# Two places where TensorE waits for a split: the head of the down projections, and the attended parts of the cross attention, taken in another order

## The chip, the cores and the metric

The kernel runs on one core of one Trainium2 chip. The time is device microseconds (us) of one execution on that core, as the median of three runs.

## The reference

512 tokens of width 1024 go through two blocks of two layers each; all data are float32. What matters here is the feed-forward part of each of the four layers and the cross attention of the last two:

```
# first block, for l in range(2)
up = h2 @ w_up[l]; a, v = up[..., :2816], up[..., 2816:]
x = x + (gelu(causal_depthwise_conv(a, conv_w[l], conv_b[l])) * v) @ w_down[l]

# second block, for layer in range(2)
q = h @ wq;  k, v = split(mem_n @ wkv)              # 4 heads of 128; 256 memory rows
p = softmax(einsum('bshd,bmhd->bhsm', q, k) * 128 ** -0.5)
x = x + einsum('bhsm,bmhd->bshd', p, v).reshape(B, S, 512) @ wo
g, u = split(h @ w_gate_up);  x = x + (silu(g) * u) @ w_down
```

## The kernel before

**Products.** Activations lie feature-major: a tile is 128 features x 512 tokens. To keep float32 accuracy at the speed of the shorter format, every operand is split in two: hi, a rounded copy, and lo, the rest. `product` (L706) makes three matmuls for each tile of the contraction, hi x hi, lo x hi and hi x lo (L711 to L713), all into one PSUM bank. M is a set of four such banks, M0 to M3, and A another.

**Weights** come in chunks. SyncE loads a chunk into `stage` (two parts); ScalarE makes w_hi (`split_hi`, L1500, the activation at L1507) when the chunk two before has been used (`w_used`), and VectorE makes w_lo (`split_lo`, L2118, at L2122). w_lo's end (`w_lo_done`) lets TensorE start (`chunk_in`, L732) and lets SyncE load the next chunk into the freed part of `stage`. Chunks alternate between two slots for their halves w_hi and w_lo, and between the banks M0, M1 and M2, M3. `m_free` tells that a bank pair was read out. The order of work on each engine is the order of the code; nothing else sets it.

**Feed-forward** (L828 on TensorE, L1630 on ScalarE, L2233 on VectorE). The 22 hidden tiles are done in two halves, of 12 and of 10. In a half, each up chunk gives one tile of each branch in two banks. VectorE scales both (L2242, L2244), the convolution runs on ScalarE and VectorE (L1640, L2252; not in layers 2 and 3), VectorE makes the w_lo of a later chunk, ScalarE the activation, VectorE the product `hid` (L2260), ScalarE `hid_hi` (L1651), and VectorE `hid_lo` (L2262), which counts up `hid_lo_done`. Then eight down chunks follow, one for each of the 8 output tiles, over the half's 12 or 10 hidden tiles: even ones into M0, odd ones into M2. In the first of them `hidden_as_split` waits for each hidden tile's hid_lo; the last hidden tile is the last of its contraction. When a down chunk is used, VectorE adds its bank to x (L2269, or L2206 in second halves, where squares for the next norm and the split of x follow), and the weights two chunks on are split.

**Cross attention** (L1138, L1833, L2609; layers 0 and 1 of the second block, whose feed-forward parts are the kernel's layers 2 and 3). Four heads. For each: scores (`score`), the row maxima and `normalise` on VectorE, the exponentials `exps` on ScalarE (L1850), the transposes `turn` (L1165) of the probabilities on TensorE, their copy `back` (L1858), and `value` (L1173), whose result is split by ScalarE (`attended_hi`, L1864) and VectorE (`attended_lo`, L2650, counting up `at_out`) into xo_hi and xo_lo. The output projection is made of parts: `part(n, k)` is head k's share of output pair n, six matmuls. Heads 0 and 1 are in the banks A while heads 2 and 3 use the banks M. TensorE's order around the change is value(0), value(1), turn(2), part(0, 0), part(0, 1), turn(3), part(1, 0), part(1, 1), value(2), value(3), and the rest of the parts. The parts with n = 2 and 3 use the second output chunk, whose w_lo VectorE makes in this stretch (`split_after(c0 + 1, 1)`).

Of the kernel before, what the change touches and what calls it, by code (L numbers as in the profile page):

```python
# [33 lines left out]
KT = D // P  # L34
# [132 lines left out]
def block_program(nc, dram, out):  # L167
# [7 lines left out]
    for l in range(2 * DEPTH):  # L175
        for half, (_, n) in enumerate(HALVES):
            c0, count = start[f"down{l}{half}"]
            size[c0:c0 + count] = [n // 2 * P] * count

    with ExitStack() as ctx:  # L180
# [524 lines left out]
        def _(pe):  # L705
            def product(bank, lhs, rhs, k, k0=0, k1=None):  # L706

                last = None
                for n in range(k0, k if k1 is None else k1):
                    (a_hi, a_lo), (b_hi, b_lo) = lhs(n), rhs(n)  # L710
                    pe.matmul(bank, a_hi, b_hi, start=(n == 0), stop=False)  # L711
                    pe.matmul(bank, a_hi, b_lo, start=False, stop=False)  # L712
                    last = pe.matmul(bank, a_lo, b_hi, start=False, stop=(n == k - 1))  # L713
                return last
# [17 lines left out]
            def chunk_in(c):  # L732

                pe.wait_ge(w_lo_done, c * 2 + 2)
                pe.wait_ge(m_free, c + 1)
# [83 lines left out]
            def turn_result(k):  # L819

                pe.wait_ge(normed_done, normed_tiles_before(LAST_NORM) + k + 1)
                if k >= 2:
                    pe.wait_ge(out_ready, k - 1)
                for t in range(TT):
                    last = pe.transpose(A[k % 2][:, t * P:(t + 1) * P], gained[:, k % 2, t * P:(t + 1) * P], ident)
                last.then_inc(out_turned, 1)

            def feed_forward(l, n_norm):  # L828
                for half, (f0, n) in enumerate(HALVES):
                    c0 = start[f"up{l}{half}"][0]  # L830
                    if half == 0:
                        normed_tiles(f"up{l}0", n_norm)
                    else:
                        with pe.Fori(0, n // 2) as i:
                            for s in range(2):
                                two_tiles(i * 2 + (c0 + s), s, normal, KT)
                    c0 = start[f"down{l}{half}"][0]

                    def down_weight(s):
                        def at(k):  # L840
                            o = (k // (n // 2)) * HALF + (k % (n // 2)) * P
                            return w_hi[:, s, o:o + P], w_lo[:, s, o:o + P]
                        return at

                    def hidden_as_split(k):

                        pe.wait_ge(hid_lo_done, up_counts(l, half) + k + 1)
                        return hidden(k)
                    if half == 1 and l == 2 * DEPTH - 1:
                        for j in range(KT):  # L850
                            chunk_in(c0 + j)
                            product(M[2 * (j % 2)][:, :], down_weight(j % 2), hidden if j else hidden_as_split, n).then_inc(w_used, 1)
                            if j:
                                turn_result(j - 1)
                        break
                    chunk_in(c0)
                    product(M[0][:, :], down_weight(0), hidden_as_split, n).then_inc(w_used, 1)
                    chunk_in(c0 + 1)
                    product(M[2][:, :], down_weight(1), hidden, n).then_inc(w_used, 1)
                    with pe.Fori(1, KT // 2) as i:  # L860
                        for s in range(2):
                            chunk_in(i * 2 + (c0 + s))
                            product(M[2 * s][:, :], down_weight(s), hidden, n).then_inc(w_used, 1)
# [635 lines left out]
        def _(act):  # L1499
# [333 lines left out]
            def cross_attention(l):  # L1833

                n0 = AT0[f"x{l}"]
                c0 = start[f"xkv{l}"][0]
                split_after(c0, 0)
                split_after(c0 + 1, 1)
                norm_rows(XATTN[l])
                split_after(c0 + 2, 0)  # L1840
                split_after(c0 + 3, 1)
                c0 = start[f"xq{l}"][0]
                split_after(c0, 0)

                def exps(h):

                    act.wait_ge(at_max, n0 + h + 1)
                    for i in range(TT):
                        j = 4 * (h % 2) + i
                        last = act.activation(x_prob[:, h % 2, i * N_MEM:(i + 1) * N_MEM], cross_scores(h, i), ACT.Exp,  # L1850
                                              bias=neg_max[:, j:j + 1], scale=P ** -0.5, accum_out=soft_den[:, j:j + 1])
                    last.then_inc(at_exp, 1)

                def back(h):

                    act.wait_ge(at_turned, n0 + h + 1)
                    for kt in range(N_MEM // P):
                        last = act.activation(x_turned[:, h % 2, kt * S:(kt + 1) * S], cross_banks[h][kt][:, :], ACT.Copy)  # L1858
                    last.then_inc(at_back, 1)

                def attended_hi(h):

                    act.wait_ge(at_pv, n0 + h + 1)
                    act.activation(xo_hi[:, h, :], cross_banks[h][0][:, :], ACT.Copy).then_inc(at_hi, 1)  # L1864

                exps(0)
                exps(1)
                back(0)
                back(1)
                split_after(c0 + 1, 1)  # L1870
                exps(2)
                exps(3)
                attended_hi(0)
                attended_hi(1)
                back(2)
                back(3)
                attended_hi(2)
                attended_hi(3)
                o0 = start[f"xo{l}"][0]
                for n in range(4):  # L1880
                    if n % 2:
                        split_hi(o0 + n // 2 + 2, n // 2)
                    if n < 2:
                        act.wait_ge(xo_added, 2 * l + n + 1)
                    else:
                        act.wait_ge(m_free, o0 + n + 1)
                    for m in range(2):
                        squared(FFN[l], 2 * n + m, m)
                        gained_hi(FFN[l], 2 * n + m)
                norm_rows(FFN[l])  # L1890
                feed_forward(2 + l, "silu", MIX[1] if l == 0 else LAST_NORM)
# [225 lines left out]
        def _(dve):  # L2117
# [8 lines left out]
            def split_after(c, s):  # L2126
                if c + 2 < chunks:
                    split_lo(c + 2, s, size[c + 2])
# [480 lines left out]
            def cross_attention(l):  # L2609
# [51 lines left out]
                maxima(2)  # L2661
                maxima(3)
                normalise(2)
                split_after(c0 + 1, 1)
                attended_lo(0)
                attended_lo(1)
                normalise(3)
                attended_lo(2)
                attended_lo(3)
                o0 = start[f"xo{l}"][0]  # L2670
# [349 lines left out]
```

## Time and profile before

| | |
|---|---|
| median of three runs | 2816.53 us |
| lowest and highest run | 2813.05 and 2818.16 us |
| span of the profiled execution, first to last instruction | 2808.1 us |
| around that span, if the profiled execution took the median | 8.4 us |
| TensorE matmuls, busy | 2745.4 us (98%) |
| VectorE, busy | 1535.5 us (55%) |
| ScalarE, busy | 1110.5 us (40%) |
| mean granted clock of TensorE | 0.994 |

The profile is of one execution, and its own whole time isn't listed beside its span; so sums are made against the span, and what lies around it is taken as the difference to the median.
### The profile page before, as it was taken

To read this page: it belongs to the slowest core of one execution; us is meant where nothing else is said; L and a number is where in the kernel's file an instruction comes from. 1 tells how busy PE (TensorE), PEld (TensorE's weight loads), DVE (VectorE), ACT (ScalarE), POOL (GpSimd) and SP (SyncE) were. 2 spreads that over 40 slices of the span, in tenths; PEclk is the share of its full clock that TensorE was granted. 3 is DMA by queue.
4 is the path that set the end of the run, shared out by engine and by line. 5 is a ranking of instruction groups with operands and counts; after the bars stand their busy time and mean duration, and the time that the engine had idled before them with its cause. 6 is when DMAs were issued, how large, how long until landed. Compare 5 with 4: busy or idle time off the path is not lost.

```text
span 2808.1 us, 33678 instructions
## 1 busy us (share of the span) xinstructions
PE 2745.4 (98%) x12745; PEld 2242.2 (80%) x12745; DVE 1535.5 (55%) x2107; ACT 1110.5 (40%) x1521; POOL 42.7 (2%) x36
## 2 busy tenths in 40 slices
PE   8999999999999999999999999999999889999998
PEld 7887788887888778888788878888878568788886
DVE  5376855456536685544667654434663545644444
ACT  3246544334313644433442443322443644533223
POOL 3000000000200000000000000000000000000000
PEclk9999999999999999999999999999999999999999
DMA  5321233332332123333243423333332114232332
GB/s 160 90 64 57 85 96 86 101 97 85 102 97 76 45 72 94 105 90 105 79 120 90 128 68 91 93 101 99 95 90 62 31 57 124 60 101 86 105 86 86
DMA packets 463902, 249.89 MB, mean 89 GB/s; under 512 B 21094, under 2 KB 459327, under 8 KB 463679
## 3 DMA queue, kind: packets, MB, share of 16 engines
q1 hardware_dynamic: 463807, 248.57, 30.9%
q8 instruction: 66, 1.08, 0.2%
q14 instruction: 29, 0.24, 0.0%
HBM read 246.44 MB, written 2.10 MB: 89 GB/s over the span
## 4 chain that ended last, share of the span: by engine, by line
PE 88%; DVE 6%; ACT 3%; issue 1%; DMA 1%; DVEq 0%; ACTq 0%; SPq 0%
PE M L711 26%; PE M L713 25%; PE M L712 25%; DVE w_lo L2122 1%; PE M L806 1%; PE M L804 1%; PE M L805 1%; PE A L901 1%; PE A L711 1%; PE A L876 1%; PE A L712 1%; PE A L713 1%; PE A L945 1%; PE A L890 0%; DVE prob L2565 0%
## 5 line engine op out<-in xcount | busy, mean ns | idle before, releaser
L711 PE MATMUL M<-h_hi,w_hi 128*128 128x512 f32 x2184 | 861.2, 394 | 3.6 <-DVE w_lo L2122 2.3
L713 PE MATMUL M<-h_hi,w_lo 128*128 128x512 f32 x2184 | 851.8, 390 | 0.0
L712 PE MATMUL M<-h_lo,w_hi 128*128 128x512 f32 x2184 | 851.7, 390 | 0.0
L1507 ACT ACTIVATE w_hi<-stage 128x1024 fp32r<-128x1024 f32 (+3 forms) x504 | 495.7, 1026 | 732.6 <-PE M L713 665.6
L2122 DVE TENSOR_TENSOR w_lo<-stage,w_hi 128x1024 fp32r<-128x1024 f32 (+3 forms) x504 | 586.8, 1202 | 149.9 <-ACT w_hi L1507 148.9
L711 PEld LDWEIGHTS M<-h_hi,w_hi 128*128 128x128 f32 x2184 | 410.8, 188 | 95.3 <-issue 5.9
L713 PEld LDWEIGHTS M<-h_hi,w_lo 128*128 128x128 f32 x2184 | 410.6, 188 | 86.7
L712 PEld LDWEIGHTS M<-h_lo,w_hi 128*128 128x128 f32 x2184 | 410.7, 188 | 86.4 <-issue 2.6
L711 PE MATMUL M<-hid_hi,w_hi 128*128 128x512 f32 x704 | 275.2, 391 | 7.0 <-DVE hid_lo L2262 7.0
L712 PE MATMUL M<-hid_lo,w_hi 128*128 128x512 f32 x704 | 274.0, 389 | 0.0
L713 PE MATMUL M<-hid_hi,w_lo 128*128 128x512 f32 x704 | 274.0, 389 | 0.0
L2242 DVE TENSOR_TENSOR normed<-M,rstd 128x512 f32<-128x512 f32 x88 | 60.9, 692 | 306.0 <-PE M L713 280.1
L711 PEld LDWEIGHTS M<-hid_hi,w_hi 128*128 128x128 f32 x704 | 132.1, 188 | 36.6 <-DVE hid_lo L2262 9.6
L713 PEld LDWEIGHTS M<-hid_hi,w_lo 128*128 128x128 f32 x704 | 132.2, 188 | 27.7
L712 PEld LDWEIGHTS M<-hid_lo,w_hi 128*128 128x128 f32 x704 | 132.1, 188 | 27.1
L1651 ACT ACTIVATE hid_hi<-hid 128x512 f32 x88 | 55.6, 632 | 180.8 <-DVE hid L2260 180.8
L2269 DVE TENSOR_TENSOR x<-x,M 128x512 f32 (+1 forms) x40 | 27.5, 688 | 165.0 <-PE M L713 165.0
L1648 ACT ACTIVATE acted<-normed 128x512 f32<-128x512 f32 x44 | 27.8, 632 | 223.8 <-DVE normed L2242 223.8
L2262 DVE TENSOR_TENSOR hid_lo<-hid,hid_hi 128x512 f32 x88 | 61.0, 693 | 82.6 <-ACT hid_hi L1651 82.6
L1640 ACT ACTIVATE conv<-normed,vec 128x512 f32<-128x512 f32 x44 | 35.9, 817 | 140.4 <-DVE normed L2242 140.2
L2252 DVE SCALAR_TENSOR_TENSOR conv<-normed,vec,conv 128x511 f32<-128x511 f32 x88 | 66.1, 751 | 46.2 <-ACT conv L1640 39.9
L2206 DVE TENSOR_TENSOR x<-x,M 128x512 f32 (+1 forms) x53 | 35.1, 683 | 85.0 <-PE M L713 83.5
(491 smaller groups left out, 3235.4 us busy)
## 6 DMA issues: line engine op xcount, KB each, us to landing
stage<-in_w_up SPq DMA_DIRECT2D x88, 512.0 KB, 4.5
stage<-in_ffn_w_gate_up SPq DMA_DIRECT2D x88, 512.0 KB, 4.8
stage<-in_w_in SPq DMA_DIRECT2D x80, 512.0 KB, 4.5
stage<-in_w_down SPq DMA_DIRECT2D x32, 384.0 KB, 3.8
stage<-in_ffn_w_down SPq DMA_DIRECT2D x32, 384.0 KB, 3.7
stage<-in_od_w_in SPq DMA_DIRECT2D x21, 512.0 KB, 4.1
stage<-in_w_down SPq DMA_DIRECT2D x32, 320.0 KB, 3.5
stage<-in_ffn_w_down SPq DMA_DIRECT2D x32, 320.0 KB, 3.4
```

The source lines that it names most:

```text
L711: pe.matmul(bank, a_hi, b_hi, start=(n == 0), stop=False)
L712: pe.matmul(bank, a_hi, b_lo, start=False, stop=False)
L713: last = pe.matmul(bank, a_lo, b_hi, start=False, stop=(n == k - 1))
L804: pe.matmul(bank, a_hi, b_hi, start=(j == 0), stop=False)
L1507: act.activation(w_hi[:, s, part * HALF:part * HALF + n], stage[:, part, 0:n], ACT.Copy)\
L1640: act.activation(conv[:, s, :], branch_in[:, s, :], ACT.Identity, bias=col_at("conv_b", i * 2 + (l * FT + f0 + s)), scale=col_at(f"conv_w{ ...
L1651: act.activation(hid_hi[:, i * 2 + s, :], hid[:, s, :], ACT.Copy).then_inc(hid_hi_done, 1)
L2122: dve.tensor_tensor(w_lo[:, s, part * HALF:part * HALF + n], stage[:, part, 0:n], w_hi[:, s, part * HALF:part * HALF + n].bitcast(F32), AL ...
L2206: added = dve.tensor_tensor(x[:, k + m, :], x[:, k + m, :], bank[:, :], ALU.add)
L2242: dve.tensor_tensor(branch_in[:, s, :], M[2 * s][:, :], rstd[:, :], ALU.mult)\
L2252: dve.scalar_tensor_tensor(conv[:, s, back:], branch_in[:, s, 0:S - back], col_at(f"conv_w{l}", i * 2 + (tap * FT + f0 + s)), conv[:, s, b ...
L2262: dve.tensor_tensor(hid_lo[:, i * 2 + s, :], hid[:, s, :], hid_hi[:, i * 2 + s, :].bitcast(F32), ALU.subtract)\
```

## The change

Two edits, without a new instruction or wait.

1. `feed_forward` on TensorE: in all eight down projections, the first four tiles of the second chunk (into M2) come between the last but one and the last tile of the first chunk (into M0). The wait for the second chunk's weights (`chunk_in(c0 + 1)`) moves ahead with them. The last projection's loop, which is written apart since it turns results beside, now begins at its third chunk.
2. `cross_attention`, two layers: ScalarE takes attended_hi(0) between exps(2) and exps(3) instead of behind exps(3); VectorE takes the split of the second output chunk behind normalise(3) instead of ahead of attended_lo(0).

```diff
--- before.py
+++ after.py
@@ -846,17 +846,19 @@
 
                         pe.wait_ge(hid_lo_done, up_counts(l, half) + k + 1)
                         return hidden(k)
+                    chunk_in(c0)
+                    product(M[0][:, :], down_weight(0), hidden_as_split, n, 0, n - 1)
+                    chunk_in(c0 + 1)
+                    product(M[2][:, :], down_weight(1), hidden, n, 0, 4)
+                    product(M[0][:, :], down_weight(0), hidden_as_split, n, n - 1, n).then_inc(w_used, 1)
+                    product(M[2][:, :], down_weight(1), hidden, n, 4, n).then_inc(w_used, 1)
                     if half == 1 and l == 2 * DEPTH - 1:
-                        for j in range(KT):
+                        turn_result(0)
+                        for j in range(2, KT):
                             chunk_in(c0 + j)
-                            product(M[2 * (j % 2)][:, :], down_weight(j % 2), hidden if j else hidden_as_split, n).then_inc(w_used, 1)
-                            if j:
-                                turn_result(j - 1)
+                            product(M[2 * (j % 2)][:, :], down_weight(j % 2), hidden, n).then_inc(w_used, 1)
+                            turn_result(j - 1)
                         break
-                    chunk_in(c0)
-                    product(M[0][:, :], down_weight(0), hidden_as_split, n).then_inc(w_used, 1)
-                    chunk_in(c0 + 1)
-                    product(M[2][:, :], down_weight(1), hidden, n).then_inc(w_used, 1)
                     with pe.Fori(1, KT // 2) as i:
                         for s in range(2):
                             chunk_in(i * 2 + (c0 + s))
@@ -1869,8 +1871,8 @@
                 back(1)
                 split_after(c0 + 1, 1)
                 exps(2)
+                attended_hi(0)
                 exps(3)
-                attended_hi(0)
                 attended_hi(1)
                 back(2)
                 back(3)
@@ -2661,10 +2663,10 @@
                 maxima(2)
                 maxima(3)
                 normalise(2)
-                split_after(c0 + 1, 1)
                 attended_lo(0)
                 attended_lo(1)
                 normalise(3)
+                split_after(c0 + 1, 1)
                 attended_lo(2)
                 attended_lo(3)
                 o0 = start[f"xo{l}"][0]
```

TensorE at the head of the first down projection (layer 0, 12 tiles), before: the last hidden tile (the three rows into M0) and what comes behind it. M0 and M2 are the banks.

```order
L711 MATMUL M0<-hid_hi,w_hi 128x512 [waits hid_lo_done]
L712 MATMUL M0<-hid_lo,w_hi 128x512
L713 MATMUL M0<-hid_hi,w_lo 128x512
L711 MATMUL M2<-hid_hi,w_hi 128x512 [waits m_free,w_lo_done]
L712 MATMUL M2<-hid_lo,w_hi 128x512
L713 MATMUL M2<-hid_hi,w_lo 128x512
```

Now; the end of the second chunk's fourth tile, the first chunk's last tile, and on:

```order
L711 MATMUL M2<-hid_hi,w_hi 128x512
L712 MATMUL M2<-hid_lo,w_hi 128x512
L713 MATMUL M2<-hid_hi,w_lo 128x512
L711 MATMUL M0<-hid_hi,w_hi 128x512 [waits hid_lo_done]
L712 MATMUL M0<-hid_lo,w_hi 128x512
L713 MATMUL M0<-hid_hi,w_lo 128x512
L711 MATMUL M2<-hid_hi,w_hi 128x512
```

The tile that waits for hid_lo_done has moved behind 12 matmuls into M2, and the wait for w_lo_done of the second chunk stands ahead of those.

ScalarE in the cross attention of layer 0, before: x_prob from the banks M is exps(2) and exps(3), xo_hi from A is attended_hi(0) and (1).

```order
L1858 ACTIVATE x_turned<-A 128x512 x4
L1507 ACTIVATE w_hi<-stage 128x1024 x2
L1850 ACTIVATE x_prob,soft_den<-M,neg_max 128x256 x8
L1864 ACTIVATE xo_hi<-A 128x512 x2
L1858 ACTIVATE x_turned<-M 128x512 x4
L1864 ACTIVATE xo_hi<-M 128x512 x2
```

Now:

```order
L1860 ACTIVATE x_turned<-A 128x512 x4
L1509 ACTIVATE w_hi<-stage 128x1024 x2
L1852 ACTIVATE x_prob,soft_den<-M,neg_max 128x256 x4
L1866 ACTIVATE xo_hi<-A 128x512
L1852 ACTIVATE x_prob,soft_den<-M,neg_max 128x256 x4
L1866 ACTIVATE xo_hi<-A 128x512
L1860 ACTIVATE x_turned<-M 128x512 x4
L1866 ACTIVATE xo_hi<-M 128x512 x2
```

attended_hi(0) has moved between the two exps. (Lines behind the first edit count two higher in the changed file.)

VectorE in the same place, before: the reciprocal and x_prob are normalise(2) and (3), w_lo is the split, xo_lo is attended_lo.

```order
L2640 RECIPROCAL soft_den<-soft_den 128x4
L2644 TENSOR_SCALAR x_prob<-x_prob,soft_den 128x256 x4
L2122 TENSOR_TENSOR w_lo<-stage,w_hi 128x1024 x2
L2650 TENSOR_TENSOR xo_lo<-A,xo_hi 128x512 x2
L2640 RECIPROCAL soft_den<-soft_den 128x4
L2644 TENSOR_SCALAR x_prob<-x_prob,soft_den 128x256 x4
L2650 TENSOR_TENSOR xo_lo<-M,xo_hi 128x512 x2
```

Now:

```order
L2642 RECIPROCAL soft_den<-soft_den 128x4
L2646 TENSOR_SCALAR x_prob<-x_prob,soft_den 128x256 x4
L2652 TENSOR_TENSOR xo_lo<-A,xo_hi 128x512 x2
L2642 RECIPROCAL soft_den<-soft_den 128x4
L2646 TENSOR_SCALAR x_prob<-x_prob,soft_den 128x256 x4
L2124 TENSOR_TENSOR w_lo<-stage,w_hi 128x1024 x2
L2652 TENSOR_TENSOR xo_lo<-M,xo_hi 128x512 x2
```

The split has moved behind both attended_lo and normalise(3).

## Rows read from the trace of the kernel before

**Rows 1.** The page, part 1: busy us, share of the span, instructions by engine.

```profile
PE 2745.4 (98%) x12745; PEld 2242.2 (80%) x12745; DVE 1535.5 (55%) x2107; ACT 1110.5 (40%) x1521; POOL 42.7 (2%) x36
```

**Rows 2.** Waits of TensorE by releaser: total us, times, longest us.

```profile
PE M L711 <- DVE hid_lo L2262: 7.0, 6, 2.0
...
PE A L711 <- DVE xo_lo L2650: 3.7, 2, 1.9
```

**Rows 3.** Timeline of TensorE, layer 0, second half: start us, us, engine, instruction.

```profile
678.32 0.39 PE L712 MATMUL M<-hid_lo,w_hi 128*128 128x512 f32 x1
678.55 0.39 PE L713 MATMUL M<-hid_hi,w_lo 128*128 128x512 f32 x1
680.90 0.50 PE L711 MATMUL M<-hid_hi,w_hi 128*128 128x512 f32 x1 [1.97 <-DVE hid_lo L2262]
...
681.48 0.40 PE L713 MATMUL M<-hid_hi,w_lo 128*128 128x512 f32 x1
```

**Rows 4.** Timeline of VectorE and ScalarE in the same stretch.

```profile
676.25 2.35 DVE L2122 TENSOR_TENSOR w_lo<-stage,w_hi 128x1024 fp32r<-128x1024 f32 x2
...
680.16 0.69 DVE L2262 TENSOR_TENSOR hid_lo<-hid,hid_hi 128x512 f32 x1 [0.95 <-ACT hid_hi L1651]
...
681.92 2.01 ACT L1507 ACTIVATE w_hi<-stage 128x1024 fp32r<-128x1024 f32 x2 [0.63 <-PE M L713]
...
683.01 2.36 DVE L2122 TENSOR_TENSOR w_lo<-stage,w_hi 128x1024 fp32r<-128x1024 f32 x2 [0.29 <-ACT w_hi L1507]
```

**Rows 5.** Timeline of TensorE at three more waits for hid_lo.

```profile
505.92 0.50 PE L711 MATMUL M<-hid_hi,w_hi 128*128 128x512 f32 x1 [0.57 <-DVE hid_lo L2262]
...
1397.33 0.50 PE L711 MATMUL M<-hid_hi,w_hi 128*128 128x512 f32 x1 [1.97 <-DVE hid_lo L2262]
...
1985.26 0.50 PE L711 MATMUL M<-hid_hi,w_hi 128*128 128x512 f32 x1 [0.91 <-DVE hid_lo L2262]
```

**Rows 6.** Timeline of TensorE, cross attention of layer 0, then of layer 1.

```profile
1638.01 3.60 PE L1173 MATMUL A<-x_turned,v_x 128*128 128x512 f32 x8
1641.44 1.04 PE L1165 MATMUL M<-const,x_prob 128*128 128x128 f32 x8
1644.35 0.47 PE L711 MATMUL A<-xo_hi,w_hi 128*128 128x512 f32 x1 [1.87 <-DVE xo_lo L2650]
...
1652.44 1.02 PE L1173 MATMUL M<-x_turned,v_x 128*128 128x512 f32 x2
...
2407.65 1.03 PE L1165 MATMUL M<-const,x_prob 128*128 128x128 f32 x8
2408.44 0.48 PE L711 MATMUL A<-xo_hi,w_hi 128*128 128x512 f32 x1
```

**Rows 7.** Timelines of ScalarE, then of VectorE, cross attention of layer 0.

```profile
1639.82 0.48 ACT L1850 ACTIVATE x_prob<-M,neg_max 128x256 f32<-128x256 f32 x1
...
1641.62 1.12 ACT L1864 ACTIVATE xo_hi<-A 128x512 fp32r<-128x512 f32 x2
...
1641.24 2.35 DVE L2122 TENSOR_TENSOR w_lo<-stage,w_hi 128x1024 fp32r<-128x1024 f32 x2
1643.52 1.28 DVE L2650 TENSOR_TENSOR xo_lo<-A,xo_hi 128x512 fp32r<-128x512 f32 x2
...
1644.92 1.14 DVE L2644 TENSOR_SCALAR x_prob<-x_prob,soft_den 128x256 f32<-128x256 f32 x4
```

**Rows 8.** Windows: stretch, its us, busy us (instructions) by engine, TensorE's granted clock, DMA.

```profile
678.00:680.00 2.00, 0.94 (x5) 0.43 (x3) 1.21 (x2) 0.63 (x2) 0.00 (x0) 1.00 0.47 143
...
368.00:372.00 4.00, 4.00 (x20) 3.30 (x19) 4.00 (x6) 2.76 (x5) 0.00 (x0) 1.00 0.39 111
...
1646.00:1647.00 1.00, 1.00 (x4) 0.81 (x3) 0.06 (x1) 0.00 (x0) 0.00 (x0) 0.50 1.01 276
...
2404.00:2405.00 1.00, 1.00 (x4) 0.81 (x3) 0.94 (x4) 0.00 (x0) 0.00 (x0) 0.50 0.97 285
```

**Rows 9.** The page, part 6: loads of 320 KB pieces, us to landing.

```profile
stage<-in_w_down SPq DMA_DIRECT2D x32, 320.0 KB, 3.5
```

## The prediction

> **What bounds the kernel now.** I read four views, in this order. First the page: TensorE is busy for 2745.4 of 2808.1 us [rows 1], so a change saves time only where it removes time in which TensorE stands still or runs slow. Then the waits of TensorE, added up by releaser: the tail of the hidden split, hid_lo at L2262, costs 7.0 us in 6 waits, and the tail of the attended split, xo_lo at L2650, costs 3.7 us in 2 [rows 2]. These are the waits which the diff is about. Then the timeline of one down projection's head, on TensorE [rows 3] and on the two engines that feed it [rows 4]; the reader is to see there what TensorE waits for and how much the rows behind the wait could have covered. Last the timeline of the cross attention [rows 6, 7], and the granted clock in short stretches [rows 8].
>
> **Head of a down projection.** There are eight (four layers, two halves); six of them wait. Take layer 0, second half (10 tiles). Matmuls start 0.23 us apart (678.32, 678.55), so tile 9 was due at 678.78. It started at 680.90, when hid_lo (680.16, 0.69 long) was done [rows 3, 4]: 2.12 us late. Its third matmul started at 681.48, where full pace would have had it at 679.24: 2.24 us lost, 0.27 more than the 1.97 of idle time that the row names, since the pipeline starts anew. The other waits have idle times of 0.57 to 1.97 [rows 5]. With 0.27 for each, the six cost 7.0 + 6 x 0.27 = 8.6 us.
>
> The change puts four tiles of the second chunk, 12 matmuls, ahead of that last tile: 12 x 0.227 = 2.7 us of work against at most 2.12 us of lateness. In the example they run from 678.78 to 681.50, and hid_lo is there at 680.85. The cover needs the second chunk's weights: their w_lo ends at 676.25 + 2.35 = 678.60 [rows 4], 0.2 us before the first of the 12 is due. That is tight in the second halves of layers 0 and 1, whose waits are the 1.97 ones; w_lo ends 2.25 us before hid_lo does, whatever the wait, so where the wait is shorter the 12 matmuls are due later and the margin is as much wider. So I take the **whole 8.6 us**; its bounds are 7.0 (idle time alone) and 8.9 (the matmuls just behind each wait run a little slow too). The two heads without a wait (first halves of layers 2 and 3) gain nothing.
>
> What the move makes late: the first chunk's w_used now rises when only 8 tiles (first halves) or 6 tiles (second halves) of the second chunk are left, where before a whole chunk was. That signal releases the addition to x, the split of the third chunk (ScalarE w_hi, VectorE w_lo) and, through the freed staging buffer, SyncE's load of the fourth. ScalarE starts 0.44 us behind the tile's third matmul (681.48 to 681.92), and w_lo ends at 683.01 + 2.36 = 685.37, so the third chunk is ready 3.9 us after that matmul [rows 3, 4]. Behind it stand 6 x 0.68 = 4.1 us of matmuls in a second half and 5.4 us in a first half. It fits, with 0.2 us left in the three second halves whose pieces are full size; in the last one the pieces are 640 wide and shorter. The third chunk's own load is issued when the second chunk's halves are split (about 677.4 and 678.6), and takes 3.5 us [rows 9]: 682.1, while ScalarE would turn to the second half at about 683.4. The fourth chunk: load issued at 3.9 us after the matmul, landed at 7.4, split by 9.7, wanted at 4.3 + 6.8 = 11.1 us. Cost taken: 0, from 0 to 0.3 us at each of three heads. In the last projection the loop is only written anew: turn_result(0) stands behind both chunks as before.
>
> The new order also changes the bank more often (M0, M2, M0, M2). The trace has that already: first_tiles changes banks every three matmuls, and the stretch 368 to 372, which is such a one, has TensorE busy throughout at a granted clock of 1.00 [rows 8]. I cost it at 0. The Trainium skill says otherwise of a like case: in TensorE: Matmul & The Clock Gate, section "A second HAM failure mode: psum-queue depth-cycling", a kernel that cycles through PSUM banks pauses so often between groups that its clock swings between the two levels. By it each head would lose instead of gain (rival 4); by the row the term is 0, and the trace doesn't agree with the rule here, as no pause comes with the change of bank.
>
> **Cross attention, twice.** Before, VectorE did normalise(2), then the split of the second output chunk (1641.24, 2.35 us), then both xo_lo (from 1643.52), while TensorE, done with turn(2), waited for the first xo_lo until 1644.35 [rows 6, 7]. Now, step by step:
> - ScalarE: value(0) is the first four of eight instructions from 1638.01, 0.43 us apart, so it is read at about 1639.9. That is where exps(3) began (1639.82). attended_hi(0) takes about 0.6 of its place, exps(3) runs from 1640.4 for its 1.8 (1639.82 to 1641.62), attended_hi(1) from 1642.25 to 1642.85.
> - VectorE: xo_lo(0) takes the split's place, 1641.24 to 1641.93. xo_lo(1) waits for ScalarE and runs 1642.88 to 1643.6. Queued behind that wait is normalise(3), which waits for exps(3) anyway; it ends at 1644.8 (before, 1646.06). The split follows, 1644.8 to 1647.2.
> - TensorE: turn(2) starts at 1641.44 as before and takes 0.79 to the next start (2407.65 to 2408.44 is the same step at full clock). The first part therefore starts at 1642.23 and not at 1644.35: **2.1 us**. The second part is due at 1643.65 and its xo_lo is there at 1643.6; turn(3) is due at 1645.05 and its input is there at 1644.8. No new wait, but margins of 0.1 and 0.2 us.
> - The split is first wanted by part(2, 0), behind value(2) and value(3) (8 x 0.43 us) and 24 matmuls: 1648.7 + 3.4 + 5.4 = 1657.5, so 10 us of cover. SyncE's next two loads start 3.5 us later; ScalarE takes them only behind part(1, 3), so they have several us to spare.
>
> Then the clock. Right behind this wait, TensorE's granted clock falls to its lower level, 1.2 GHz (0.50 in 1646 to 1647, and in 2404 to 2405 after the other layer's wait) [rows 8]. From 1644.35 to the next value(2) at 1652.44 go 8.09 us [rows 6]; at full clock it would be 24 matmuls x 0.227 + 0.79 + three restarts of 0.1 = 6.5. So the slow spell costs **1.6 us** in each layer. Behind the 1.97 us of idle time in 678 to 680 the clock stays at 1.00 [rows 8], so such a wait doesn't always bring the fall; but with the wait gone TensorE works without a break from 1634 on, and I take the spell as gone too. Bounds: 0 and 1.6. Sum for two layers: 2 x (2.1 + 1.6) = 7.4 us.
>
> **Sum.** 8.6 + 7.4 = 16.0 us. Span 2808.1 - 16.0 = 2792.1. The median of the runs, 2816.53, is 8.4 above the profiled span; with the same 8.4 on top: **2800.5 us** (-0.57%). A measurement of this kernel can tell about 0.2%, 5.6 us, from no change; its own three runs lie 5.1 us apart.
>
> **Rivals.**
> 1. The slow spell stays or moves. The clock falls after waits of 1.87 us here and not after 1.97 there, so something besides the wait's length counts. If both spells stay in some form, 3.2 us are kept: 2803.7. And since every later wait falls at another moment than before, one of those may bring a fall that it didn't bring; each costs some 1.6. The Trainium skill (same page, section "What's actually happening") has it that the monitor behind the clock runs free and that the moment of a change differs from run to run; no single profile can show that. Chance 0.17.
> 2. The third chunk is late. If w_lo comes 0.5 us later than I work out, the three full-size second halves each wait 0.3 to 0.6 us, and the margins of 0.1 and 0.2 in the attention go as well: 2 to 3 us less gain, 2803. For it: a load that lands later than 3.5 us. Against: ScalarE's two w_hi ran back to back there [rows 4]. Chance 0.08.
> 3. The change doesn't do what it says: time saved on TensorE comes back as waits for weights, since loads set the pace. Then 2811 to 2816, within 0.2%. Against: TensorE's waits name VectorE, and every load is released by a split, so it moves with TensorE. Chance 0.04.
> 4. Slower. The change of banks at the head of each down projection (a place where it never was) brings the clock to its lower level for a spell. A spell like that behind the attention costs 1.6 us, eight of them 12.8: 2813. It is slower than before from 2.0 us at each head on, and at two spells per head it is 26 us: 2826. Against it stands the 1.00 of the first_tiles stretch. Chance 0.02.
> The forecast keeps 0.69.
>
> **How the numbers follow.** Forecast 0.69 (own range 2797 to 2803, from 8.9 and 7.0 at the heads and half the runs' spread), with rivals 1 and 2 up to 2806. I give 2796 to 2806.5; it leaves out rivals 3 and 4 and the tails. Faster by over 0.2% is below 2810.9: the forecast, rivals 1 and 2: 0.94. Within 0.2%: 0.04. Slower: 0.02.
>
> **What would show it.** Right: the wait for hid_lo is gone from TensorE's waits, or below 0.5 us; at the head the 12 matmuls start 0.23 us after tile 8 and the last tile follows without idle time; the first xo part starts 0.8 us behind turn(2); no stretch below 1.00 between turn(2) and value(2). Wrong: TensorE waiting for w_lo at the second chunk (cover not ready) or at the third (rival 2); a granted clock below 1.00 at a head (rival 4) or still behind turn(2) (rival 1); waits for xo_lo or x_prob at part(0, 1) or turn(3). A gain under 10 us would mean that a term, and not only a size, is wrong.

## The result, and the profile after

| | before | after |
|---|---|---|
| median of 5 runs of each | 2818.16 us | 2799.81 us |
| lowest and highest | 2813.05, 2819.13 | 2797.49, 2803.30 |
| profiled span | 2808.1 us | 2795.3 us |

The ratio is 0.9941, with a 95% interval from 0.9929 to 0.9953: 16.6 us of 2816 (13 to 20), faster. Forecast were 2800.5 us and a gain of 16.0 us.

The first line of the page of after stands against [rows 1]: TensorE's busy time is the same within 0.3 us, in a shorter span. Then the waits of TensorE in after (total us, times, longest us), which answer to [rows 2].

```profile
PE 2745.1 (98%) x12745; PEld 2244.1 (80%) x12745; DVE 1535.6 (55%) x2107; ACT 1112.3 (40%) x1521; POOL 40.6 (1%) x36
```

```profile
PE A L1032 <- DMA rows<-in_norm: 6.5, 1, 6.5
PE M L711 <- DVE w_lo L2124: 4.8, 5, 2.3
PE M L1398 <- DVE m_prob L2954: 4.3, 2, 3.6
```

No line for hid_lo and none for xo_lo is left in the whole list, and no new one has come. (Line numbers are two higher than before from the down projection on.)

**The head of a down projection**, layer 0, second half, on TensorE in after; it answers to [rows 3]. The rows are the first of the 12 matmuls moved ahead, the second and third of the first chunk's last tile, and the one behind it. The second chunk's w_lo is done at 675.67 + 2.35 = 678.02, 0.2 us before the 12 start.

```profile
678.20 0.40 PE L711 MATMUL M<-hid_hi,w_hi 128*128 128x512 f32 x1
...
681.16 0.39 PE L712 MATMUL M<-hid_lo,w_hi 128*128 128x512 f32 x1
681.39 0.39 PE L713 MATMUL M<-hid_hi,w_lo 128*128 128x512 f32 x1
681.62 0.39 PE L711 MATMUL M<-hid_hi,w_hi 128*128 128x512 f32 x1
```

VectorE, then ScalarE, in the same stretch; they answer to [rows 4].

```profile
675.67 2.35 DVE L2124 TENSOR_TENSOR w_lo<-stage,w_hi 128x1024 fp32r<-128x1024 f32 x2
...
679.58 0.69 DVE L2264 TENSOR_TENSOR hid_lo<-hid,hid_hi 128x512 f32 x1 [0.95 <-ACT hid_hi L1653]
...
682.91 2.36 DVE L2124 TENSOR_TENSOR w_lo<-stage,w_hi 128x1024 fp32r<-128x1024 f32 x2 [0.30 <-ACT w_hi L1509]
...
681.82 2.01 ACT L1509 ACTIVATE w_hi<-stage 128x1024 fp32r<-128x1024 f32 x2 [1.11 <-PE M L713]
```

hid_lo is done at 680.27, and TensorE runs on at its pace of 0.23 us; the last tile's third matmul starts at 681.39. In [rows 3] it starts at 681.48, and there the 12 matmuls are still to come. ScalarE takes the third chunk's weights 0.43 us behind that matmul, and w_lo ends at 685.27. The six tiles left end with the pace at 681.62 + 6 x 0.68 = 685.70, so the third chunk is ready 0.4 us early, and TensorE doesn't wait.

From the first matmul of the first chunk to the first of the third, the eight heads took 17.19, 15.90, 17.37, 15.91, 16.32, 14.80, 16.32 and 15.17 us before, and 16.32, 13.62, 16.32, 13.63, 16.32, 13.60, 16.32 and 13.96 after: 128.98 and 120.09, **8.9 us less**.

**Cross attention**, layer 0, on TensorE in after, against [rows 6]:

```profile
1633.26 3.60 PE L1175 MATMUL A<-x_turned,v_x 128*128 128x512 f32 x8
1636.69 1.04 PE L1167 MATMUL M<-const,x_prob 128*128 128x128 f32 x8
1637.49 0.47 PE L711 MATMUL A<-xo_hi,w_hi 128*128 128x512 f32 x1
...
1640.36 1.03 PE L1167 MATMUL M<-const,x_prob 128*128 128x128 f32 x8
...
1643.97 3.59 PE L1175 MATMUL M<-x_turned,v_x 128*128 128x512 f32 x8
```

And the two engines that feed it, VectorE and then ScalarE, against [rows 7]:

```profile
1636.50 0.68 DVE L2652 TENSOR_TENSOR xo_lo<-A,xo_hi 128x512 fp32r<-128x512 f32 x1
1638.12 0.69 DVE L2652 TENSOR_TENSOR xo_lo<-A,xo_hi 128x512 fp32r<-128x512 f32 x1 [0.94 <-ACT xo_hi L1866]
...
1638.93 1.14 DVE L2646 TENSOR_SCALAR x_prob<-x_prob,soft_den 128x256 f32<-128x256 f32 x4
1639.99 2.35 DVE L2124 TENSOR_TENSOR w_lo<-stage,w_hi 128x1024 fp32r<-128x1024 f32 x2
...
1635.18 0.60 ACT L1866 ACTIVATE xo_hi<-A 128x512 fp32r<-128x512 f32 x1
...
1637.47 0.62 ACT L1866 ACTIVATE xo_hi<-A 128x512 fp32r<-128x512 f32 x1
```

Measured from turn(2)'s start at 1636.69, the first part starts 0.80 behind it (forecast 0.79), xo_lo(1) 1.43 (1.44), and normalise(3) ends 3.38 behind it (3.36). From turn(2) to value(2) it was 11.00 us [rows 6] and is now 1643.97 - 1636.69 = 7.28; the same in layer 1 (10.95 and 7.27): **7.4 us less** for the two.

Windows of after (stretch, its us, busy us and instructions by engine in the order PE, PEld, DVE, ACT, POOL, then TensorE's granted clock, DMA), against [rows 8]: the whole stage is at full clock, and so is the head with its three changes of bank.

```profile
1632.00:1640.00 8.00, 8.00 (x34) 5.28 (x33) 6.41 (x19) 6.88 (x22) 0.00 (x0) 1.00 0.00 0
1640.00:1648.00 8.00, 8.00 (x34) 5.34 (x33) 3.04 (x4) 2.09 (x4) 0.00 (x0) 1.00 0.46 132
678.00:682.00 4.00, 4.00 (x19) 3.29 (x18) 1.88 (x5) 2.10 (x3) 0.00 (x0) 1.00 0.60 164
```

So the two places gave 8.9 + 7.4 = 16.3 us, but the two profiled spans differ by only 12.8. The other 3.5 us were lost where nothing was changed. With the two profiles laid side by side, after is 0.3 us longer up to the first down projection, 1.3 between layer 0's second head and layer 1's first, 0.6 between layer 2's second head and the second cross attention, 1.2 behind the last head, and 0.1 in all the rest. In each of these four stretches TensorE had the lower clock for longer than before: 6.8 us instead of 3.4 near 224, 3.4 us at 739 where there was none, 6.8 instead of 3.4 near 2200, and 11.2 instead of 8.7 at the end. Added up over the whole span it was 32.6 us before, 6.8 of them behind the attention, and 38.5 us in after, none of them there. That these spells wander between executions of like code, the experiments show.

### The profile page after: what moved, and what is told of

Its sections match the earlier page's. It is cut to its first block, busy times and chain, and to the rows that moved or that the text cites. A ratio compares the mean times of both kernels' runs of the same rounds, so it can differ in the third digit from the quotient of the medians.

```text
span 2795.3 us, 33678 instructions
## 1 busy us (share of the span) xinstructions
PE 2745.1 (98%) x12745; PEld 2244.1 (80%) x12745; DVE 1535.6 (55%) x2107; ACT 1112.3 (40%) x1521; POOL 40.6 (1%) x36
## 4 chain that ended last, share of the span: by engine, by line
PE 91%; DVE 5%; ACT 3%; issue 1%; DMA 0%; SPq 0%; ACTq 0%; DVEq 0%
PE M L711 26%; PE M L713 26%; PE M L712 26%; DVE w_lo L2124 1%; PE M L805 1%; PE M L806 1%; PE M L804 1%; PE A L903 1%; PE A L947 1%; PE A L878 1%; PE A L711 1%; PE A L712 0%; PE A L713 0%; PE A L892 0%; DVE prob L2567 0%
```

## The experiments

The theory: the two parts of the change are independent and each gives what its stage shows. The rivals: the slow clock behind the attention isn't tied to its wait; and the cross attention's gain comes from one of its two moves alone. Times are given as a difference to the kernel before on the same chip, from the ratio and its 95% interval.

**1. The down projections alone.** The attention is left as it was before.

```diff
                 exps(2)
-                attended_hi(0)
                 exps(3)
+                attended_hi(0)
```
```diff
                 normalise(2)
+                split_after(c0 + 1, 1)
                 attended_lo(0)
                 attended_lo(1)
                 normalise(3)
-                split_after(c0 + 1, 1)
```

> The first edit alone (down projections); the cross attention stays as before. If the two edits add up, as I hold: 8.9 us less than before (8.9 is what the six heads lose between the first and the third chunk in the trace), the six waits for hid_lo gone, both waits for xo_lo (3.7 us) and the slow spells behind them still there. The rival, that the heads' gain comes back later as other waits and most of the total is due to the attention, gives under 4 us less.

Measured: 0.9964 (0.9951 to 0.9978), 10.1 us less (6 to 14). The heads take 120.09 us again. The waits for xo_lo are back as in [rows 2], but without a spell behind them. TensorE in the attention, and the windows there:

```profile
1641.51 1.04 PE L1167 MATMUL M<-const,x_prob 128*128 128x128 f32 x8
1644.41 0.47 PE L711 MATMUL A<-xo_hi,w_hi 128*128 128x512 f32 x1 [1.86 <-DVE xo_lo L2652]
```

```profile
1646.00:1648.00 2.00, 2.00 (x14) 1.69 (x13) 0.13 (x1) 0.00 (x0) 0.00 (x0) 1.00 0.87 242
1648.00:1650.00 2.00, 2.00 (x12) 1.67 (x11) 0.00 (x0) 1.09 (x2) 0.00 (x0) 1.00 0.04 11
```

The same wait, 1.86 against 1.87 us, and the clock stays at 1.00. From turn(2) to value(2) it takes 9.37 and 9.34 us in the two layers. So the wait costs 9.35 - 7.28 = 2.1 us in each layer, as forecast, and a spell, where it comes, 11.0 - 9.35 = 1.65 us, the size forecast. What was wrong is that it always comes.

**2. Filling the wait.** Of kernel 1, with seven matmuls in front of part(0, 0) whose result is overwritten: TensorE works where it stood still, and nothing starts earlier.

```diff
                 pe.wait_ge(w_lo_done, o0 * 2 + 1)
+                for _ in range(7):
+                    pe.matmul(A[1][:, :], w_hi[:, 0, 0:P], h_hi[:, 0, :], start=True, stop=True)
                 part(0, 0)
```

> As e1_down_only, and seven more 128x512 matmuls (1.6 us at full clock) between turn(2) and the wait for the first xo_lo, into a bank that part(0, 0) then overwrites; nothing that is kept depends on them. They fill most of the 1.87 us wait, and don't shorten it. If TensorE's standing still is what brings the slow clock behind the wait: no stretch below 1.00 there, and 3.2 us less than e1_down_only. If the kind of work ahead of the wait brings it (the float32 values and the transposes) or the loads that start there: granted clock 0.50 as before, and the time of e1_down_only.

Measured: 0.9959 (0.9945 to 0.9972), 11.5 us less, within the interval of kernel 1. From turn(2) to value(2) it takes 9.30 us in both layers, at full clock. Since kernel 1 had no spell there either, this tells nothing on the clock. It does show that the wait's own 2.1 us are not got back by keeping TensorE busy: 0.15 us of idle time is left of the 1.87, and the first part starts 2.81 us behind turn(2), where it was 2.90.

**3. The cross attention alone.** The diff's two moves in the attention, made to the kernel before; VectorE's is that of kernel 4 below, and ScalarE's is this:

```diff
                 exps(2)
+                attended_hi(0)
                 exps(3)
-                attended_hi(0)
```

> The second edit alone (cross attention, both engines). If the edits add up: 7.4 us less than before, of which 4.2 for the two waits and 3.2 for the two slow spells; from the start of turn(2) to the start of value(2) 7.3 us, not 11.0. If the spells are only moved elsewhere by it: 4.2 us less, with granted clocks below 1.00 at two new places.

Measured: 0.9979 (0.9970 to 0.9988), 5.9 us less (3 to 8). Turn(2) to value(2) takes 7.29 and 7.28 us; the waits for hid_lo are those of [rows 2], 7.0 us in 6. Windows of this kernel behind the 1.97 us wait in layer 0, second half:

```profile
680.00:682.00 2.00, 0.90 (x3) 0.78 (x4) 1.18 (x2) 1.46 (x2) 0.00 (x0) 0.93 0.65 194
682.00:684.00 2.00, 2.00 (x6) 1.55 (x5) 1.30 (x2) 1.71 (x2) 0.00 (x0) 0.50 0.04 13
684.00:686.00 2.00, 2.00 (x7) 1.54 (x7) 2.00 (x3) 1.43 (x3) 0.00 (x0) 0.72 0.03 9
```

Here the clock falls where it did not in [rows 8], with the same code and the same wait, and that head takes 17.48 us instead of 15.90: 1.6 us again.

**4. VectorE's move alone,** the split behind normalise(3), ScalarE as before:

```diff
                 normalise(2)
-                split_after(c0 + 1, 1)
                 attended_lo(0)
                 attended_lo(1)
                 normalise(3)
+                split_after(c0 + 1, 1)
```

> Only VectorE's part of the second edit: the split behind normalise(3); attended_hi(0) stays behind exps(3). The first xo_lo then ends at about 1642.9 on the clock of the trace of before, and TensorE waits 0.7 us less 0.25 instead of 1.87. If the split is what made it late: 1.4 us less in each layer, and 1.6 more if the slow spell goes with the longer wait: 6.0 us less than before in all. If ScalarE's order was the bound: 0 to 1 us less.

Measured: 0.9988 (0.9979 to 0.9997), 3.4 us less (1 to 6). Turn(2) to value(2) takes 8.12 us in both layers, with a wait left, since xo_hi still stands behind exps(3):

```profile
1648.09 0.47 PE L711 MATMUL A<-xo_hi,w_hi 128*128 128x512 f32 x1 [0.65 <-DVE xo_lo L2650]
```

The expectation of 6.0 was too high, just outside the interval: it counted both spells as a sure gain. Against 9.35 us without a spell the move is worth 1.2 us a layer, 2.5 in all. What a spell in a part of the executions adds is worked out in the next section. Behind the 0.65 us left there was none in either layer.

**5. ScalarE's move alone,** the diff shown with kernel 3, VectorE as before.

> Only ScalarE's part of the second edit: attended_hi(0) between exps(2) and exps(3); VectorE's split stays ahead of attended_lo(0). VectorE ends that split 1.2 us after either order of ScalarE has xo_hi(0) ready, so nothing is gained: within 0.5 us of before, and the waits for xo_lo still 1.9 us each. If ScalarE's order was half of the cause: 2 to 3 us less.

Measured: 1.0002 (0.9992 to 1.0012): nothing that can be told from zero, within 3 us either way, as expected. VectorE reads the first xo_hi only behind its split, so an earlier xo_hi helps nobody. The two moves are thus not additive: 0, 1.2, and 2.1 us a layer together. TensorE and the windows in layer 0:

```profile
1646.14 0.47 PE L711 MATMUL A<-xo_hi,w_hi 128*128 128x512 f32 x1 [1.87 <-DVE xo_lo L2650]
```

```profile
1648.00:1650.00 2.00, 2.00 (x6) 1.56 (x5) 0.00 (x0) 0.00 (x0) 0.00 (x0) 0.50 0.75 204
```

The spell is there in this layer; layer 1 of the same execution takes 9.34 us and has none.

**6. Seven tiles instead of four** of the second chunk ahead of the last one:

```diff
-                    product(M[2][:, :], down_weight(1), hidden, n, 0, 4)
+                    product(M[2][:, :], down_weight(1), hidden, n, 0, 7)
...
-                    product(M[2][:, :], down_weight(1), hidden, n, 4, n).then_inc(w_used, 1)
+                    product(M[2][:, :], down_weight(1), hidden, n, 7, n).then_inc(w_used, 1)
```

> The changed kernel with seven tiles of the second chunk ahead of the last one, not four: five (first halves) or three (second halves) are left behind it, 3.4 or 2.0 us, against 3.9 us until the third chunk's w_lo is ready. If that margin is what limits the cover, as I hold: waits for w_lo at the third chunk of 1.7 us in three second halves, 0.7 in the last, 0.3 in the first halves; with 0.27 for each restart 9 us more than the changed kernel. If the third chunk has more room than that: the time of the changed kernel.

Measured: 0.9984 (0.9974 to 0.9994), 4.5 us less than before. The waits of TensorE, and the third chunk of layer 0, second half:

```profile
PE M L711 <- DVE w_lo L2124: 10.8, 12, 2.3
```

```profile
689.24 0.49 PE L711 MATMUL M<-hid_hi,w_hi 128*128 128x512 f32 x1 [1.59 <-DVE w_lo L2124]
```

The heads take 16.80, 15.37, 16.81, 15.36, 16.80, 15.35, 16.79 and 14.73 us: 128.01 in all, 7.9 more than with four tiles. The expectation was 9 us more than the kernel after; by the ratios it is 12.1 (8 to 17), which the 7.9 at the heads account for in part. Three tiles fewer behind the last one are 3 x 0.68 = 2.0 us of cover less. With the margin of 0.4 us that the profile of after shows, the wait should be 1.6 us, and the row has 1.59; with the 0.2 us of the prediction it would be 1.8. By this margin a fifth tile, 0.68 us, would already cost something in a second half, and four would be the largest number that doesn't; five and six were not run.

**7. One tile instead of four:**

```diff
-                    product(M[2][:, :], down_weight(1), hidden, n, 0, 4)
+                    product(M[2][:, :], down_weight(1), hidden, n, 0, 1)
...
-                    product(M[2][:, :], down_weight(1), hidden, n, 4, n).then_inc(w_used, 1)
+                    product(M[2][:, :], down_weight(1), hidden, n, 1, n).then_inc(w_used, 1)
```

> The changed kernel with one tile ahead, not four: 0.68 us of cover against 0.7 to 2.1 us of lateness. Left over: 1.4 us at each of the two long waits, 0.05 to 0.4 at the other four, 3.9 us in all, and 0.27 for each restart: 5 us more than the changed kernel. If one change of order were enough and the number of tiles didn't count: its time.

Measured: 0.9965 (0.9953 to 0.9977), 9.9 us less than before. The wait for hid_lo is partly back:

```profile
PE M L711 <- DVE hid_lo L2264: 3.0, 4, 1.3
```

The heads take 124.80 us, 4.7 more than with four tiles, where 5 were expected; by the ratios it is 6.8 (2 to 12). The banks change as often as with four tiles, three times at each head, and 3.0 of the 4.7 us are idle time for hid_lo; the other 1.7 are 0.3 us at each of the six heads, about what a restart behind a wait costs. Kernels 6 and 7 bracket the number of tiles: the work in front of the last tile has to cover 2.1 us of lateness, and the work behind it the 3.9 us of the third chunk's weights.

**8. The same idea in the next place.** With the two waits gone, the list names m_prob (3.6 us, one wait) and w_lo (2.3 us) in the latent attention, where the last head's scores are turned. TensorE in after:

```profile
2276.03 1.26 PE L1398 MATMUL A<-const,m_prob 128*128 128x128 f32 x10
2282.30 2.38 PE L1398 MATMUL M<-const,m_prob 128*128 128x128 f32 x10 [3.64 <-DVE m_prob L2954]
2305.06 0.50 PE L711 MATMUL M<-h_hi,w_hi 128*128 128x512 f32 x1 [2.29 <-DVE w_lo L2124]
2317.72 1.91 PE L1129 MATMUL A<-const,mem_tok 128*128 128x128 f32 x16
```

The second one is 2.38 us long for ten small products, where the first takes 1.26: the clock is low, and it is low again behind the second wait. Windows of after:

```profile
2282.00:2284.00 2.00, 1.70 (x8) 1.71 (x9) 0.24 (x1) 0.00 (x0) 0.00 (x0) 0.59 0.00 0
...
2306.00:2308.00 2.00, 2.00 (x7) 1.56 (x6) 1.60 (x3) 0.04 (x1) 0.00 (x0) 0.56 1.00 292
```

The edit, on top of after, puts parts of the output projection that are ready ahead of that turn:

```diff
-            turn(MLA_HEADS - 1)
             pe.wait_ge(w_lo_done, o0*2 + 4)
-            for k in range(4):
+            pe.wait_ge(at_back, n0 + MLA_HEADS - 1)
+            for k in range(3):
                 out_part(1, k)
+            turn(MLA_HEADS - 1)
+            out_part(1, 3)
+            out_part(0, 5)
             values(MLA_HEADS - 1)
-            for n, k in ((0, 5), (0, 6), (1, 4), (1, 5), (1, 6), (0, 7), (1, 7)):
+            for n, k in ((0, 6), (1, 4), (0, 7), (1, 5), (1, 6), (1, 7)):
                 out_part(n, k)
```

> The changed kernel, with the same idea at a third place: three of the four parts of the second output chunk ahead of turn(7) of the latent attention, which waits 3.6 us for its probabilities; one of them and a part of the first chunk between turn(7) and values(7); and the first output chunk's last part two parts earlier, so that the third chunk's w_lo (waited for 2.3 us, too) starts sooner. If these waits go and the slow spells behind them: 3.6 + 2.3 + 2 x 1.6 + 0.5 = 9.6 us less than the changed kernel. If the first wait moves to values(7) (copies of turn(7) not ready in time): 2 us less gain.

Measured: 0.9920 (0.9904 to 0.9936), 22.5 us less than before, median 2792.85 us. By the ratio it is the fastest of all kernels here. TensorE in the same place, and the windows:

```profile
2283.02 1.26 PE L1398 MATMUL A<-const,m_prob 128*128 128x128 f32 x10
2289.95 1.25 PE L1398 MATMUL M<-const,m_prob 128*128 128x128 f32 x10
2315.36 1.91 PE L1129 MATMUL A<-const,mem_tok 128*128 128x128 f32 x16
```

```profile
2284.00:2296.00 12.00, 11.90 (x65) 8.71 (x63) 2.54 (x9) 4.76 (x14) 0.00 (x0) 1.00 0.01 1
...
2306.00:2316.00 10.00, 10.00 (x48) 8.31 (x48) 4.93 (x7) 3.61 (x5) 0.00 (x0) 1.00 0.55 159
```

The last turn no longer waits, the two spells of the stretch are gone with its waits, and from the one turn to the memory's transposes it takes 32.34 us instead of 41.69: 9.35 less, where 9.6 were expected. The gain over after is 5.9 us by the ratios, with an interval of about 0 to 12, so the total can't tell 9.35 from less. In the profile, 7.0 us had been lost ahead of this place: up to 2270 us the lower clock lasted 27.3 us against 20.5 in after, up to 3.4 us of time, and TensorE waited 3.1 us at 757 us, for a reason of its own (last section).

## Why the prediction was right

**The heads.** Forecast 8.6 us with bounds of 7.0 and 8.9; measured 8.9 from one profile to the other, at the upper bound. The idle time is 7.0 of it [rows 2], and the other 1.9 are 0.31 us for each of the six restarts, where 0.27 was forecast. In layer 0, second half, it is 15.90 - 13.62 = 2.28 against 2.24. The two heads without a wait gained nothing, as said.

**What the move makes late.** Right: no wait came at the second or third chunk. The 3.9 us from the matmul to the third chunk's w_lo was right (3.88), but the 4.1 us of cover left out the matmul itself; the margin is 0.4 and not 0.2 us. Kernel 6 measures the same from the other side. The load and the fourth chunk showed nothing, as costed.

**The change of banks.** Costed at 0 by the row of a like stretch; the clock is 1.00 at this head, and the heads take what their matmuls need at full pace (72 x 0.227 = 16.3 and 60 x 0.227 = 13.6 us; only the very last takes 13.96). The Trainium skill (TensorE: Matmul & The Clock Gate, section "A second HAM failure mode: psum-queue depth-cycling") tells of a kernel that cycled through PSUM banks, paused briefly between its groups of matmuls, and had its clock swing between the two levels. In this kernel it does not swing: no pause comes with the change.

**The attention's wait.** 2.1 us a layer forecast, 2.1 measured (kernel 1 against after), and the three steps compared above within 0.02 us. Margins of 0.1 and 0.2 us at part(0, 1) and turn(3) were 0.15 and 0.3, and held.

**The clock: the term that was mis-sized.** The prediction took 1.6 us per layer as sure behind the attention's waits, and nothing behind the heads' waits, since the one profile showed it so. The size of a spell is right (1.65 and 1.6), the certainty was not. The profiles of before and of kernels 1, 3, 4 and 5 together have 14 such waits of 1.86 to 1.97 us:

| wait | how often | spell behind it |
|---|---|---|
| xo_lo, attention (before, kernels 1 and 5) | 6 | 3 |
| hid_lo, layers 0 and 1, second half (before, kernels 3, 4 and 5) | 8 | 3 |
| the same places with the wait removed, attention (after, kernels 3, 6, 7 and 8) | 10 | 0 |
| the same places with the wait removed, heads (after, kernels 1, 2, 6 and 8) | 10 | 0 |

Six of 14, in no relation to the code: the same wait at the same place has a spell in one profile and none in another. Shorter idle times at these stages, of 0.65 us (kernel 4, twice), 1.3 (kernel 7, twice) and 1.59 (kernel 6, three times), had none behind them. Each of the long waits then costs 0.43 x 1.6 = 0.7 us on average on top of itself. For the attention that is 1.4 us instead of 3.2, and the heads' two long waits carry another 1.4 that the prediction left at nothing. With that, kernel 1 should gain 8.9 + 1.4 = 10.3 (10.1 measured), kernel 3, the attention alone, 4.1 + 1.4 = 5.5 (5.9), and the whole 15.8 (16.6). By the same count kernel 4 should gain 2.5 + 1.4 = 3.9 (3.4). So there were two errors of nearly the same size and opposite sign, and the total was right partly by luck. This rests on the count, and fourteen cases give the share only roughly. The times alone can't tell it: the intervals of kernels 1 and 3 hold the prediction's 8.6 and 7.4 too, and only kernel 4 speaks against sure spells, by a hair. The granted clocks of all runs point the same way without settling it: 11 runs of kernel 3 had the lower clock for 37.2 us on average and 21 runs of before for 40.7, which is 3.5 us less, give or take 4; by the share it would be 2.9, with two sure spells 6.8. That the spells hang on these waits rests on the 20 places without a wait that had none; why the clock falls behind one wait and not behind its twin stays open.

Rival 1, a spell that stays or moves, is right as a mechanism: other spells did come and go (32.6 us at the lower clock before, 38.5 after, 34.2 to 51.4 in the profiles of the experiments). Over several runs it kept no 3.2 us: that would have left a gain of 12.8, and the interval begins at 13. Rivals 2, 3 and 4 didn't occur. Kernel 6 shows what rival 2 would have been.

**The time around the span.** The prediction put 8.4 us on top of its span. The profiled run of after took 2797.49 us with a span of 2795.3: 2.2 us lie around a span. So the profiled execution of before, with 2.2 us around it too, took about 2810.3 us and was itself 6 us faster than the median of its runs; only 2.2 of the 8.4 lie around the span. The predicted time isn't touched by this, since it is the median less the sum. The predicted span of 2792.1 us, 3.2 below the profiled one, was a span for an execution as fast as that one.

## What to carry to other kernels

Where an engine waits at a fixed place for the last small piece of a chain, put ready work from the next step ahead of it, and bracket the amount from both sides: work in front must cover the lateness, work left behind must cover what the late release sets off. Two engines' moves on one chain are worth nothing one by one where the other still holds the piece back; cost them together. One profile can't tell a sure cost from a likely one: a slow-clock spell behind a short wait should be entered with a share, and the span of a single execution be compared with the median only after its fixed surround is known.

## What the runs showed of the hardware that was not expected

**The clock.** A wait of 1.9 us was followed by a spell of 3.4 us at 1.2 GHz in 6 of 14 cases, so each such wait was dearer by 0.7 us on average than it looks. Idle time isn't the only thing that precedes a spell: in after the clock also falls at 739.5, where TensorE waits for nothing and works through small matmuls (128x1, L783 and L786). Windows of after:

```profile
738.00:740.00 2.00, 2.00 (x11) 2.00 (x11) 0.00 (x0) 0.00 (x0) 2.00 (x3) 0.88 0.00 0
740.00:742.00 2.00, 2.00 (x4) 0.97 (x5) 0.00 (x0) 0.00 (x0) 2.00 (x3) 0.50 0.00 0
```

**VectorE held off by GpSimd.** In the profiles of kernels 1 and 8 TensorE waits 3.1 us for w_lo at 757 us, where the other eight profiles have no wait. Kernel 1's instructions of w_lo in 736 to 757 us (least/median/longest ns), then VectorE and GpSimd (POOL) there:

```profile
L2124 DVE TENSOR_TENSOR w_lo<-stage,w_hi x2: 1211/6298/11384, 744.8 to 756.1; 128x1024 fp32r<-128x1024 f32 x2
```

```profile
744.80 12.52 DVE L2124 TENSOR_TENSOR w_lo<-stage,w_hi 128x1024 fp32r<-128x1024 f32 x2 [0.21 <-ACT w_hi L1509]
...
744.64 1.18 POOL L1496 CAST hp_hi<-h_hi 128x512 fp32r<-128x512 f32 x1
745.73 1.14 POOL L1497 CAST hp_lo<-h_lo 128x512 fp32r<-128x512 f32 x1
...
753.96 1.14 POOL L1497 CAST hp_lo<-h_lo 128x512 fp32r<-128x512 f32 x1
```

One subtraction of 1.21 us takes 11.38: it starts at 744.80 and ends at 756.18, 1.1 us after the last of GpSimd's casts (755.10). Nine casts in a row went ahead of it. In after the two take turns instead, casts of 2.1 us beside two subtractions of 2.1:

```profile
745.03 4.11 DVE L2124 TENSOR_TENSOR w_lo<-stage,w_hi 128x1024 fp32r<-128x1024 f32 x2 [0.21 <-ACT w_hi L1509]
...
745.98 2.09 POOL L1496 CAST hp_hi<-h_hi 128x512 fp32r<-128x512 f32 x1
```

The Trainium skill (SBUF — State Buffer, section "🔬 SBUF: two separate sides") has it that a VectorE instruction with two inputs in SBUF and a GpSimd instruction that reads SBUF exclude each other for a whole instruction. The rows of after agree with that; that one engine can be passed over nine times running is seen in kernels 1 and 8, 2 of 10 profiles. What decides between the two courses was not tried, nor was moving the casts elsewhere; it would be the next thing to try, since 3.1 us are at stake in those executions.
